# Half of the conditioning product moved from its own stage into the projections' first pass; silu moved ahead of the parameters' transfers

## The reference

```
def _layer(x, c, ...):
    mod = jax.nn.silu(c) @ w_ada + b_ada
    sh1, sc1, gt1, sh2, sc2, gt2 = jnp.split(mod[:, None, :], 6, axis=-1)
    h = _rmsnorm(x, g_mix) * (1 + sc1) + sh1
    proj = h @ w_in
    ...
    x = x + gt1 * mix
    h2 = _rmsnorm(x, g_ffn) * (1 + sc2) + sh2
    ...
    x = x + gt2 * ((jax.nn.silu(gconv) * u) @ f_w_down)
```

## Time and profile before

| | us |
|---|---|
| median of 3 runs | 3074.48 (3073.72 to 3075.69) |
| profiled execution, its own time | 3078.29 |
| its span (first to last instruction) | 3076.6 |

### The profile page before, as it was taken

The page is one execution under the profiler, slowest core; times in us unless marked ns, Lnnn a source line. Parts: engine busy times, 40 slices in busy tenths (PEclk is TensorE's granted clock), DMA queues, the critical chain, the costliest instruction groups (busy, mean ns, idle before and its releaser), DMA issues.

```text
span 3076.6 us, 41959 instructions
## 1 busy us (share of the span) xinstructions
PE 2849.7 (93%) x16302; PEld 2552.9 (83%) x16302; DVE 1300.1 (42%) x2489; ACT 983.0 (32%) x1682; POOL 245.7 (8%) x413
## 2 busy tenths in 40 slices
PE   3499999999777999997999999999999999999987
PEld 1288888999656888886999998799999879999965
DVE  1333333423245554544333345443334445444444
ACT  0133234423322454444222224322222433222333
POOL 0000000000024333331000000000000000000000
PEclk8699999999878999998999999999999999999998
DMA  8622224222446434334322234432222543322343
GB/s 285 227 88 90 94 89 144 83 87 71 113 156 228 132 126 133 126 112 123 102 62 63 67 92 147 157 106 80 61 61 63 163 154 112 103 75 75 102 149 120
DMA packets 324284, 355.36 MB, mean 116 GB/s; under 512 B 26470, under 2 KB 265674, under 8 KB 323702
## 3 DMA queue, kind: packets, MB, share of 16 engines
q1 hardware_dynamic: 313700, 348.52, 35.7%
q10 hardware_dynamic: 10452, 5.04, 0.7%
HBM read 285.63 MB, written 70.10 MB: 116 GB/s over the span
## 4 chain that ended last, share of the span: by engine, by line
PE 48%; DVE 2%; DMA 1%; issue 1%; ACT 0%; SPq 0%; POOL 0%; DVEq 0%; ACTq 0%
PE acc_ps L2957 14%; PE acc_ps L2914 11%; PE acc_ps L2913 11%; PE acc_ps L2915 11%; DMA f_raw<-in_f_w_down 1%; DMA f_xr<-scratch_x 0%; DVE f_y L3206 0%; DVE f_w_lo L3180 0%; ACT f_w_hi L3053 0%; DVE f_xr L3200 0%; DVE f_prod L3194 0%; DVE f_h_lo L3232 0%; DMA out_y_prompt<-f_y 0%; DVE f_w_lo L3123 0%; DVE f_mid_lo L3184 0%
## 5 line engine op out<-in xcount | busy, mean ns | idle before, releaser
L2913 PE MATMUL acc_ps<-f_h_hi,f_w_hi 128*128 128x384 f32 (+1 forms) x2112 | 689.0, 326 | 2.9 <-DVE f_w_lo L3123 2.8
L2915 PE MATMUL acc_ps<-f_h_hi,f_w_lo 128*128 128x384 f32 (+1 forms) x2112 | 688.4, 326 | 0.0
L2914 PE MATMUL acc_ps<-f_h_lo,f_w_hi 128*128 128x384 f32 (+1 forms) x2112 | 688.4, 326 | 0.0
L3123 DVE TENSOR_TENSOR f_w_lo<-f_raw,f_w_hi 128x1024 fp32r<-128x1024 f32 x242 | 296.6, 1225 | 659.2 <-ACT f_w_hi L3011 656.4
L3011 ACT ACTIVATE f_w_hi<-f_raw 128x1024 fp32r<-128x1024 f32 x242 | 257.0, 1062 | 796.7 <-PE acc_ps L2915 532.8
L2913 PEld LDWEIGHTS acc_ps<-f_h_hi,f_w_hi 128*128 128x128 f32 x2112 | 396.9, 188 | 4.2 <-DVE f_w_lo L3123 3.0
L2914 PEld LDWEIGHTS acc_ps<-f_h_lo,f_w_hi 128*128 128x128 f32 x2112 | 397.0, 188 | 0.1
L2915 PEld LDWEIGHTS acc_ps<-f_h_hi,f_w_lo 128*128 128x128 f32 x2112 | 396.8, 188 | 0.0
L2957 PE MATMUL acc_ps<-f_w_hi,f_mid_hi 128*128 128x512 f32 x748 | 237.9, 400 | 33.4 <-DVE f_mid_lo L3184 17.9
L2957 PE MATMUL acc_ps<-f_w_lo,f_mid_hi 128*128 128x512 f32 x748 | 234.7, 395 | 0.0
L2957 PE MATMUL acc_ps<-f_w_hi,f_mid_lo 128*128 128x512 f32 x748 | 234.0, 395 | 0.0
(11 more groups left out here) (503 smaller groups left out, 4165.8 us busy)
## 6 DMA issues: line engine op xcount, KB each, us to landing
f_raw<-in_f_w_down SPq DMA_DIRECT2D x122, 512.0 KB, 3.5
f_raw<-in_f_w_gate SPq DMA_DIRECT2D x66, 512.0 KB
f_raw<-in_f_w_up SPq DMA_DIRECT2D x66, 512.0 KB, 3.9
w_ada<-in_w_ada SPq DMA_DIRECT2D x12, 2048.0 KB
m_bc<-scratch_bc SPq DMA_DIRECT2D x15, 768.0 KB, 5.0
scratch_tok<-p_m SPq DMA_DIRECT2D x17, 640.0 KB, 3.0
m_tok<-scratch_tok SPq DMA_DIRECT2D x16, 640.0 KB, 5.1
scratch_ht<-p_m SPq DMA_DIRECT2D x17, 512.0 KB, 3.9
```

Of the source, the lines that this page charges most:

```text
L2913: t.matmul(dst, hi, h2_hi[:, k, cols], start=(k == 0), stop=False)
L2914: t.matmul(dst, hi, h2_lo[:, k, cols], start=False, stop=False)
L2915: last = t.matmul(dst, lo, h2_hi[:, k, cols], start=False, stop=(k == KD - 1))
L3123: v.tensor_tensor(w_lo[j][:], raw[j][:], w_hi[j][:], ALU.subtract).then_inc(s_lo[j], 1)
```

## The change

Three edits. First, `modulation` only makes the six column groups of the mixers' half, the gate's two first, then shift and scale; its tiles move into a class `Conditioning` whose memory lies under that of `projections`, so that the silu rows turned (`cond_t`), the fold and the spread matrices and two weight buffers stay valid into it. Slices of `w_in` are loaded from the second group on. Second, `projections` makes feed forward's six groups (`LATE = 6`): group q is loaded by SP at tile 2q + 1, multiplied by PE in tile 2q + 2 after its first unit, biased by DVE after that tile's layer norm, folded or spread by PE after the tile's fourth unit (the second gate row in the next tile after its first unit), and kept by DVE at the next tile's start. Both results use the PSUM bank `aux`. Since bias, sum and gate rows lie in `raw`, `load_w` of the first three slices moves from tile 10 to tile 15. Third, ACT's silu goes ahead of all of its transfers, and the relative bias's stores ahead of the parameters' transfers.

```diff
 class Conditioning:
...
+        self.tok_raw = [sb(f"w_tok_raw{j}", [P, TOK_W]) for j in range(2)]
...
+        self.w_late = [late0, late1]
+        self.mod = late0
...
 def modulation(...):
+        JS = (4, 5, 0, 1, 2, 3)
...
-            for j in range(NG):
-                if j >= 2:
-                    sp.wait_ge(s_m, j - 1)
-                    sp.wait_ge(s_mk, j - 1)
+            for i, j in enumerate(JS):
+                if i >= 2:
+                    sp.wait_ge(s_m, i - 1)
+                    sp.wait_ge(s_mk, i - 1)
...
-                if j >= NG - KD:
-                    w_in.load(sp, j - (NG - KD))
+                if i >= 1:
+                    w_in.load(sp, i - 1)
+            for k in range(NG - 1, KD):
+                w_in.load(sp, k)
+                if k == NG - 1:
                     sp.wait_ge(s_gatek, 4)
                     sp.dma_start(S["mix_gate"], gate_rows[:]).then_inc(s_gout, 16)
-            sp.wait_ge(s_gatek, 8)
-            sp.dma_start(S["ffn_gate"], gate_rows[:]).then_inc(s_gout, 16)
-            sp.wait_ge(s_gout, 32)
+            sp.wait_ge(s_gout, 16)
 
         @block.scalar
         def _(act):
+            act.wait_ge(s_in, 32)
+            nc.scalar.activation(cond, cond, ACT.Silu).then_inc(s_e, 1)
             rel_load(act)
+            rel_store(act)
...
             for dst, at in par["loads"](A):
                 act.dma_start(dst, at, allow_slow_non_contiguous=True).then_inc(s_par, 16)
-            act.wait_ge(s_in, 32)
-            nc.scalar.activation(cond[:], cond[:], ACT.Silu).then_inc(s_e, 1)
-            rel_store(act)
...
+            for i in range(NG):
+                dve.wait_ge(s_m, i + 1)
+                nc.vector.tensor_tensor(mod[:, i % 4, :], mod_ps[:, i % 2, :],
+                                        bias[:, i % 2, :], ALU.add).then_inc(s_mk, 1)
+                if i >= 2:
+                    w_in.low(nc, dve, i - 2)
...
 def projections(...):
+            def load_late(q):
+                cols = slice((6 + q) * 512, (7 + q) * 512)
+                sp.wait_ge(s_lclear, 1)
+                if q:
+                    sp.wait_ge(s_lprod, q)
+                    sp.wait_ge(s_lmod, q)
+                sp.dma_start(late_bias[0:NS], A["b_ada"][0, cols].partition_broadcast(NS)).then_inc(s_lw, 16)
+                for step in range(2):
+                    sp.dma_start(cd.w_late[step][:], late_view[:, 4 * step:4 * step + 4, cols]).then_inc(s_lw, 16)
...
                 if n >= 1:
                     store_rows(n - 1)
-                if n == 10:
+                if n % 2 and n // 2 < LATE:
+                    load_late(n // 2)
...
+                if n == LASTN - 1:
...
                     for m in range(3):
                         load_w(m)
...
+            def late_product(q):
+                pe.wait_ge(s_lw, 48 * (q + 1))
+                if q:
+                    pe.wait_ge(s_lkeep, q if q <= 4 else 2 * q - 4)
...
+                for step in range(KD // COL_GROUPS):
+                    for g in range(COL_GROUPS):
+                        last = t.matmul(aux[g * GW_PE:(g + 1) * GW_PE, :], cd.cond_t[:, step * COL_GROUPS + g, :],
+                                        cd.w_late[step][:, g, :], start=(step == 0), stop=(step == KD // COL_GROUPS - 1))
+                last.then_inc(s_lprod, 1)
...
+                    if n and n % 2 == 0 and n // 2 <= LATE:
+                        if ui == 0:
+                            late_product(n // 2 - 1)
+                        if ui == 3:
+                            late_turn(n // 2 - 1, 0)
```

More of the change, by code:

```diff
@@ L198, with __init__ @@
 class TokenWeights:
-    def __init__(self, A, sem, sb, w_hi, w_lo):
-        self.raw = [sb(f"w_tok_raw{j}", [P, TOK_W]) for j in range(2)]
+    def __init__(self, A, sem, raw, w_hi, w_lo):
+        self.raw = raw
         self.w_hi, self.w_lo = w_hi, w_lo
@@ L308, in projections @@
         s_cin, s_ct, s_ctk, s_copy = sem("p_conv_rows"), sem("p_conv_turned"), sem("p_conv_turned_kept"), sem("p_copies")
+        s_lclear, s_lw, s_lprod, s_lmod, s_lcol, s_lkeep, s_lgate = (sem("p_late_" + n) for n in (
+            "cleared", "loaded", "product", "made", "turned", "kept", "stored"))
+        LATE = 6
         s_gd, s_ga, s_gp, s_gm, s_gst = (sem("p_" + n) for n in ("gate_dve", "gate_act", "gate_pe", "gate_pool", "gate_stored"))
@@ L388, in _ @@
                     store_rows(n - 1)
[L389 removed]
+                if n % 2 and n // 2 < LATE:
+                    load_late(n // 2)
+                if n in (12, 14):
+                    for who in range(2):
+                        q = (n - 12) // 2
+                        sp.wait_ge(s_lkeep, 4 + 2 * q + who + 1)
+                        sp.dma_start(S["ffn_gate"][:, who, q * 512:(q + 1) * 512], late_gate[who]).then_inc(s_lgate, 16)
+                if n == LASTN - 1:
                     sp.wait_ge(s_f, 1)
                     sp.wait_ge(s_fk, 1)
+                    sp.wait_ge(s_lkeep, 4 + 4)
+                    sp.wait_ge(s_lgate, 16 * 4)
                     for m in range(3):
@@ L814, in _ @@
             for n in range(NTT):
+                q = (n - 3) // 2
+                if n % 2 and 0 <= q < LATE:
+                    if q < 4:
+                        late_columns(q)
+                    else:
+                        late_rows(q, 0)
                 if n + 1 < NTT:
@@ L1132, in keep_gate @@
             def keep_gate(n):
-                who, half = n % 4 // 2, n % 2
+                who, half = n // 2, n % 2
                 dve.wait_ge(s_gate, n + 1)
-                if n == 4:
-                    dve.wait_ge(s_gout, 16)
                 nc.vector.tensor_copy(gate_rows[:, who, half * 512:(half + 1) * 512], gate_ps[:, n % 4, :]
                                       ).then_inc(s_gatek, 1)
[L1140 to L1146, removed]
+            for i in range(NG):
[4 more added lines that the diff above has]
+                    w_in.low(nc, dve, i - 2)
+                if i == 2:
@@ L1160, in _ @@
-            for n in range(4, 8):
-                keep_gate(n)
+            cols = col_ps[:, 0:2 * KD * NS].rearrange("p (a k s) -> p a k s", a=2, k=KD)
+            nc.vector.tensor_copy(keep["mix_shift"][:], cols[:, 0]).then_inc(s_colk, 1)
+            nc.vector.scalar_tensor_tensor(keep["mix_scale"][:], cols[:, 1], 1.0, spread(cd.g_mix[:], 2, NS), ALU.add, ALU.mult
+                                           ).then_inc(s_colk, 1)
+            for k in range(NG - 2, KD):
+                w_in.low(nc, dve, k)
```

144 lines of the change are left out of this document (89 added, 55 removed).

## The result

| us | median | lowest to highest | runs |
|---|---|---|---|
| before | 3075.09 | 3073.72 to 3079.49 | 4 |
| changed | 3053.14 | 3049.03 to 3054.98 | 4 |

The ratio is 0.9924 with a 95% interval of 0.9907 to 0.9942, so the change saves 22.0 us (18 to 29). The forecast was 3059.5, with a range of 3047 to 3070. The profiled execution of the changed kernel took 3049.03 us, the lowest of the four, with a span of 3047.0. Times of one kernel differ by some 7 us either way from run to run, while in the profiles kept here the end of the conditioning's stage repeats within 2.4 us and the length of the first pass within 1 us; so the places in the traces are the sharper measure, and the times stand beside them.

The account below looks back on a forecast made before the run. Transfers were taken to bound `modulation` and PE the first pass. From the profiled 3078.3 us, minus 34.4 saved plus 19.4 added gives 3063.3; that execution stood 3.8 above the median, so 3059.5 us, range 3047 to 3070.

Parts of the forecast that it names:

- the wait of the first `high` behind ACT's list: In `modulation`, ACT issues slice 0's `high` behind its small transfers; q1 stands empty some 11 us, 34.4 us saved.
- From `high` to the stage's end: In `modulation`, from the first `high` at 48 us to the next stage's first load at 96: 48.0 us.
- The pass: In `projections`, PE's added six products (11.5), four folds (4.2) and four spreads (3.7) are paid in full: 19.4 us.
- the end of ACT's list: In `modulation`, ACT's `par_taps` end at 42.5 us, `more` takes 5.8, so `high` of slice 0 starts about 48.
- the time at which q1 runs dry: In `modulation`, SP's 10.2 MB ahead of its first wait for `low` are through at about 40.5 us.
- The small packets' 2.0 us: In `modulation`, q10's small packets beside q1 take 12% of the engines for about 17 us: 2.0 us.
- the relative bias was charged with 6.7 us: In `modulation`, the relative bias's 1.6 MB take 84% of all engines for 8 us, 6.7 us added to q1's time.
- One piece for one: With both queues loaded, the DMA engines send one q10 packet per q1 packet, some 176 per us each.
- Rival A: ACT's list isn't in the way, small pieces going faster than one for one: `high` near 28, 45 us saved, 3049 us; chance 0.16.
- B: ACT's list takes longer: `high` at 57 to 69, 3068.5 to 3080 us, gain only pays for PE's work; chance 0.13.
- C: Slower: PE stands for late weights after the first unit of tiles 2 to 12; 3080.5 us; chance 0.05.
- D: The change doesn't shorten `modulation`: 3093.9 us, chance nil; of silu's move alone, ACT's list takes what it gives.

Follow-up runs that it names:

- e5_product_twice: The changed kernel with each late product made a second time into the same PSUM bank; 3062.59 us, ratio 0.9960.
- e6_late_later: The changed kernel with each late group's load issued one tile later, about 3 us ahead of its product instead of 24; 3102.04 us, ratio 1.0083.
- e1_silu_back: The changed kernel with silu and the relative bias's stores back behind the parameters' transfers on ACT; 3053.97 us, ratio 0.9921.
- e0_again: The changed kernel as it is, run once more beside others on the same chip; 3054.39 us, ratio 0.9923.
- e7_spread: The changed kernel with two `high` ahead of the parameters, which are spread between later ones, none between seventh and eighth `high`; 3042.40 us, ratio 0.9895.

## Why the prediction was right

**The mechanism held step by step.** Once the 12.6 MB were gone, the wait of the first `high` behind ACT's list took over, as forecast, with the large queue empty for some 11 us (from 36.0, where the last packet of q1 starts, to the issue at 46.85; forecast 40.5 to 51.7). From `high` to the stage's end I had 48.0 us and the trace has 47.4. The pass had 19.4 and got 19.7. That this is so close is luck: e5_product_twice puts the products at 10.0 to 10.9 instead of 11.5, so the folds, spreads and the joints between them take some 9 to 10 and not 7.9. The clock in the pass is 1.00, and nothing waits for the late weights; in e6_late_later a load landed within 8.5 us of its issue (forecast 8), which here is 15 us before its use (136.24 to 160.3, forecast 14).

**The term that was mis-sized** is the end of ACT's list. I put the end of `par_taps` at 42.5 and `high` at 48; they came at 37.7 and 43.0. This gives 40.0 instead of 34.4 us of the stage, 5.6 of the 6.4 by which the time was lower than forecast; the rest is within the spread. The cause is the step before it, the time at which q1 runs dry: 36.0 and not 40.5. The queues of the changed kernel from 4 to 36 us (packets, MB, share of the 16 engines):

```profile
q1 hardware_dynamic: 5055, 10.24, 84.5%
q10 hardware_dynamic: 3833, 1.85, 20.4%
```

Of 32 us that is 27.0 and 6.5 us of the engines' time, where I had 27.8 and 6.7 + 2.0 = 8.7; and the shares add to 105%, so that 33.5 us of work took 32. Two terms were too large. The small packets' 2.0 us came on top of a pace of 368 GB/s that q1 keeps beside them (2.56 MB from 23 to 30 us, 366 GB/s, in the rows further down); in the earlier trace rows the shares already add to 110.6%, which I read as a loss of q1's. And the relative bias was charged with 6.7 us from a window in which its queue ran alone. From 17 to 23 us, beside q1, it moved 1.36 MB in 59.5% of 6 us:

```profile
q10 hardware_dynamic: 554, 1.36, 59.5%
```

That is 2.6 us for a MB and not 4.0 (6.7 by 1.68). Its pieces of 3 KB took 121 ns by the median in both windows; alone, some of them took several times as long, and the mean was 182 ns against 127.

**One piece for one** held again, with 1252 packets beside 1251 from 23 to 30 us:

```profile
q1 hardware_dynamic: 1252, 2.56, 96.5%
q10 hardware_dynamic: 1251, 0.01, 10.3%
```

Equal counts alone don't tell how an engine turns, since equal batches from both queues would give them too; that I took the earlier trace rows as evidence against such batches was a step too far. The starts of the packets in this trace do tell: from 23 to 30 us, 1107 of q1's 1252 start 6 ns after one of q10, and 746 are followed by a next one of q1 86 ns later (a piece of 2 KB takes 84 ns, a small one 9), so an engine takes one of each in turn. The Trainium skill, page "DMA: Bandwidth & Descriptors", section "Queues, rings and completion order", has an engine take some 9 to 17 descriptors of one queue before it turns; these packets don't show that. Nor would that rule by itself send many small pieces for one large, as I had derived. Rival A falls as a mechanism by the counts., which I read as q10 alone, still has q1's last 118 packets in its first us. `high` came nearer to rival A's place than I thought, because q1 was dry earlier, not because the small pieces went faster beside it.

**The rivals.** B (a longer list) is out by `high` at 43. C (PE stands for the late weights) didn't come, and e6_late_later shows what it needs, a load issued a whole tile later; its price there is 8 us for each wait of 6, clock included, so that I had priced it too low. D's sentence on silu, that ACT's list takes what the move gives, is shown by e1_silu_back for the changed kernel. It isn't so in the kernel before, where the same edit gave 6.8 us by the times and 8.3 by the traces' stage ends. The parts of this change don't add up: 22 us with the silu edit, 22.7 without it (e1_silu_back), some 7 with it alone.

**Not settled.** The changed kernel's profiled span is 29.6 us shorter than that of before, while the stage and the pass account for 20.3. The sample stage's first load is 21.8 earlier (796.97 after 818.74), as is the store behind tile 16; the other 7.8 us come later in the program, in parts that the change doesn't touch. In e0_again's profile the span is 3056.8, 19.8 shorter than before's, with the sample stage's first load at the same place (797.26). From that load to the end the two profiles of the changed kernel take 2250.0 and 2259.5 us, the two of the kernel before 2257.9 and 2253.3, so I take the 7.8 us for the spread of single executions; no run was made on what moves in it.

## What to carry to other kernels

When a stage that waits for transfers is cut, follow every queue and each engine's own order to the first instruction that the second half needs: here an issue list of 24 small transfers on ACT had been free under 55 us of waiting, and cost 9.5 us once the data came early. An edit that removes a wait can be worth 7 us in one version and nothing in the next, so it is priced in the order in which it will run. Work that is put on the engine that bounds a stage is paid almost in full (10 to 11 us for six products of 1.92), and a load that feeds it needs its lead: issued one tile later, each cost its wait and then the lower clock too.

## What the runs showed of the hardware

- An issue on ACT can stand for many microseconds while earlier transfers of its queue still have many small packets to send beside another queue: one transfer of the gains took 5.09 us, one of `par_gd` 6.17, four `par_taps` 7.97 in e7_spread. In two pairs, with nothing of their own queue ahead, the same four took 2.2 us together, the second pair in a stretch with the engines at 98%.
- From 23 to 30 us two loaded queues were served piece by piece in turn: on an engine a pair of 2 KB and 4 bytes mostly started every 86 ns, though its parts are recorded with 84 and 9, so the shares of two queues can add to 105%. The relative bias's bytes took less of the engines' time beside another queue's work than alone (2.6 against 4.0 us for a MB).
- After a wait of 6 us in a tile that is otherwise at clock 1.00, the granted clock was 0.50 for the next 3.6 us and 0.98 over the 20 behind them.
